# Fused RWKV-7 and attention blocks: moving the inversion's buffers and reordering the first loads of the recurrence

## The reference

```python
def step(S, inp):                       # per head, S is 64 x 64, for t = 1..512
    r_t, w_t, k_t, v_t, kk_t, kka_t = inp
    sa = jnp.einsum('bhvk,bhk->bhv', S, kk_t)
    S = (S * w_t[:, :, None, :] - sa[..., None] * kka_t[:, :, None, :]
         + v_t[..., None] * k_t[:, :, None, :])
    y_t = jnp.einsum('bhvk,bhk->bhv', S, r_t)
    return S, y_t
```

## Time and profile before

| what | value |
|---|---|
| median of 3 runs | 2405.3 us (2401.07 to 2406.37) |
| the profiled execution | 2402.93 us |
| its span of instructions | 2401.2 us |
| TensorE busy | 2141.7 us (89%) |
| VectorE busy | 1413.9 us (59%) |
| ScalarE busy | 1004.4 us (42%) |
| GpSimd busy | 264.8 us (11%) |
| mean granted TensorE clock | 0.955 |

### The profile page before, as it was taken

The page is one execution under the profiler, slowest core; times in us unless marked ns, Lnnn a source line. Parts: engine busy times, 40 slices in busy tenths (PEclk is TensorE's granted clock), DMA queues, the critical chain, the costliest instruction groups (busy, mean ns, idle before and its releaser), DMA issues.

```text
span 2401.2 us, 43608 instructions
## 1 busy us (share of the span) xinstructions
PE 2141.7 (89%) x16706; PEld 1664.0 (69%) x16706; DVE 1413.9 (59%) x2214; ACT 1004.4 (42%) x1768; POOL 264.8 (11%) x233
## 2 busy tenths in 40 slices
PE   3798999986888888799999999887989997999998
PEld 1576666765777776577888888575756685787876
DVE  6776776765656564446553555579855556434445
ACT  3454554443655565323222322331477424323233
POOL 2102000000222223100000000079100000000000
PEclk6899999997999999899999999899999999999998
DMA  3234445463333231332333333122211131333322
GB/s 100 70 123 133 137 142 160 154 157 84 82 81 88 67 73 38 93 91 79 87 96 98 94 94 95 58 79 61 79 53 36 40 100 53 87 97 96 96 87 80
DMA packets 395656, 217.19 MB, mean 90 GB/s; under 512 B 85104, under 2 KB 374280, under 8 KB 395272
## 3 DMA queue, kind: packets, MB, share of 16 engines
q1 hardware_dynamic: 394896, 215.13, 31.1%
q10 hardware_dynamic: 632, 0.21, 0.0%
HBM read 181.68 MB, written 33.62 MB: 90 GB/s over the span
## 4 chain that ended last, share of the span: by engine, by line
PE 62%; DVE 19%; ACT 10%; issue 6%; SPq 1%; DMA 1%; DVEq 0%; POOL 0%; ACTq 0%
PE bank L1460 16%; PE bank L1462 15%; PE bank L1461 15%; DVE w_lo L1605 4%; PE bank L512 3%; DVE dconv L1853 3%; ACT w_hi L1237 2%; PE bank L489 1%; DVE tmp L1654 1%; PE bank L520 1%; PE bank L435 1%; PE bank L421 1%; PE bank L867 1%; PE bank L463 1%; PE bank L858 1%
## 5 line engine op out<-in xcount | busy, mean ns | idle before, releaser
L1460 PE MATMUL bank<-xl,w_hi 128*128 128x512 f32 (+1 forms) x1696 | 685.2, 404 | 72.8 <-DVE xl L1610 40.8
L1461 PE MATMUL bank<-xl,w_lo 128*128 128x512 f32 (+1 forms) x1696 | 668.3, 394 | 0.0
L1462 PE MATMUL bank<-xl,w_hi 128*128 128x512 f32 (+1 forms) x1696 | 667.2, 393 | 0.0
L1237 ACT ACTIVATE w_hi<-w_raw 128x1024 fp32r<-128x1024 f32 (+2 forms) x298 | 301.6, 1013 | 438.7 <-PE bank L1462 434.1
L1460 PEld LDWEIGHTS bank<-xl,w_hi 128*128 128x128 f32 (+1 forms) x1696 | 320.5, 189 | 196.0 <-issue 62.3
L1605 DVE TENSOR_TENSOR w_lo<-w_raw,w_hi 128x1024 fp32r<-128x1024 f32 (+2 forms) x298 | 353.3, 1186 | 141.1 <-ACT w_hi L1237 129.7
L1462 PEld LDWEIGHTS bank<-xl,w_hi 128*128 128x128 f32 (+1 forms) x1696 | 321.1, 189 | 70.6 <-issue 2.4
L1461 PEld LDWEIGHTS bank<-xl,w_lo 128*128 128x128 f32 (+1 forms) x1696 | 321.6, 190 | 67.1 <-issue 4.4
L1460 PE MATMUL bank<-xh,w_hi 128*128 128x512 f32 x480 | 199.1, 415 | 49.8 <-DVE w_lo L1605 44.7
L1462 PE MATMUL bank<-xh,w_hi 128*128 128x512 f32 x480 | 193.0, 402 | 0.0
L1461 PE MATMUL bank<-xh,w_lo 128*128 128x512 f32 x480 | 192.6, 401 | 0.0
(11 more groups left out here) (310 smaller groups left out, 3091.2 us busy)
## 6 DMA issues: line engine op xcount, KB each, us to landing
w_raw<-in_a_w_in SPq DMA_DIRECT2D x64, 512.0 KB, 4.3
w_raw<-in_b_w_in SPq DMA_DIRECT2D x64, 512.0 KB, 4.0
w_raw<-in_w_ffn_up SPq DMA_DIRECT2D x44, 512.0 KB, 3.7
w_raw<-in_w_in SPq DMA_DIRECT2D x36, 512.0 KB, 3.6
w_raw<-in_a_w_out SPq DMA_DIRECT2D x16, 512.0 KB, 3.9
w_raw<-in_b_w_out SPq DMA_DIRECT2D x16, 512.0 KB, 3.8
w_raw<-in_w_ffn_down SPq DMA_DIRECT2D x16, 512.0 KB, 3.9
d_g<-sq SPq DMA_DIRECT2D x16, 256.0 KB, 2.1
```

Source lines behind the costliest of these rows:

```text
L1237: A(w_hi[0:rows, slot, 0:nkb, 0:ncol], w_raw[0:rows, slot, 0:nkb, 0:ncol], ACT.Copy).then_inc(s_hi, 1)
L1460: mm(outp, wh, xlo, start=start, stop=False)
L1461: mm(outp, wl, xhi, start=False, stop=False)
L1462: return mm(outp, wh, xhi, start=False, stop=stop)
```

## The change

The inversion's f32 buffer `nix`, and `nix16` and `inv2`, move out of the `hT` region into the second `xl` region. `tt` and `rhs` take their place in the `hT` region, where `nixlo16` and `w16` stay. ScalarE's wait for the last spill is removed, and VectorE's moves from its first instruction of the recurrence to its first write of `w16` (step 10 of pair 0). GpSimd's wait stays. In SP's queue the keys of pair 0 now stand between the two halves of its queries, and both halves of pair 1's queries move behind the values of pair 0 and `spill_mix(15)`.

```diff
         st_v = over("st_v", [P, 2, (NCH + 1) * C])
         sv = [over(f"sv{n}", [P, 2, NCH, 2, C]) for n in range(2)]
-        tt = [over(f"tt{n}", [P, 2, NCH, C]) for n in range(2)]
+        nix = [over(f"nix{a}", [P, NCH, C]) for a in range(2)]
+        nix16 = [over(f"nix16_{a}", [P, NCH, C], F16) for a in range(2)]
+        inv2 = [over(f"inv2_{a}", [P, 2, NCH, C], F16) for a in range(2)]
         st_pc = [over(f"st_pc{n}", [P, 2, NCH]) for n in range(3)]
-        rhs = over("rhs", [P, 2, C])
...
         assert spot == hT_at
-        nix = [over(f"nix{a}", [P, NCH, C]) for a in range(2)]
-        nix16, nixlo16, w16 = ([over(f"{n}_{a}", [P, NCH, C], F16) for a in range(2)]
-                               for n in ("nix16", "nixlo16", "w16"))
-
-        inv2 = [over(f"inv2_{a}", [P, 2, NCH, C], F16) for a in range(2)]
+
+        tt = [over(f"tt{n}", [P, 2, NCH, C]) for n in range(2)]
+        nixlo16, w16 = ([over(f"{n}_{a}", [P, NCH, C], F16) for a in range(2)] for n in ("nixlo16", "w16"))
+        rhs = over("rhs", [P, 2, C])
...
                     if when(t, PAIRS):
-                        if t == 0 and s == 0:
-                            act.wait_ge(s_spill, SPILL_MIX + SPILL_TILE * CI)
                         if s in (1, 3, 5, 7):
...
             dve.wait_ge(s_const, 3)
-            dve.wait_ge(s_spill, SPILL_MIX + SPILL_TILE * CI)
...
                         level = (s - S_LEVELS) // 2 + 1
+                        if t == 0 and level == 1:
+                            dve.wait_ge(s_spill, SPILL_MIX + SPILL_TILE * CI)
...
-            for half in range(2):
-                load_q(0, half)
+            load_q(0, 0)
             load_keys(0)
-            for half in range(2):
-                load_q(1, half)
+            load_q(0, 1)
             sp.wait_ge(s_unit, U_MIX + 4 * (CI - 1) + 3)
             load_values(0)
             spill_mix(CI - 1)
+            for half in range(2):
+                load_q(1, half)
             panel(U_OUT1 + 1, 1, i["a_w_out"][0], 0, KB, P)
```

## The result

| | before | changed |
|---|---|---|
| median of 6 runs each | 2405.49 us (2399.06 to 2407.77) | 2390.70 us (2386.92 to 2395.24) |
| the profiled execution | 2402.93 us | 2386.92 us |
| its span | 2401.2 us | 2385.2 us |
| TensorE busy | 2141.7 us | 2139.0 us |

The ratio of the times is 0.995, with a 95% interval of 0.9931 to 0.9969. The forecast was 2393 us with a range of 2387.5 to 2398.5.

A forecast was written before the change was run, and what follows sets the result against it. Bound: one queue and one landing decide 30.9 us into the recurrence. Terms 0 + 8.35 + 2.6 + 0 = 10.9 us gave 2392.0 against the profiled execution, 2394.4 against the median; forecast between them 2393 us, range 2387.5 to 2398.5.

The forecast's parts named there:

- The bound: From mix stage to recurrence, one queue and one landing decide 30.9 us; moving this hand-over moves the rest.
- The keys: Pair 0's key loads: first products start at about 534.4, 3.7 us earlier, and TensorE's 3.75 us idle stretch goes.
- The values: Pair 0's value loads: issued sooner, so TensorE's transposes start at 539.5, 8.35 us earlier, 2.3 us behind the last issue.
- The spill gate: ScalarE's start of the recurrence: no longer waiting for the last spill gains 2.6 us, because the values come next.
- VectorE's moved wait and pair 1's queries: VectorE's first `w16` and pair 1's query loads: both cost nothing, with covers of 16.7 us and 25 us.
- The clock: TensorE in pair 0's four groups: falls to half clock as before, 5.4 us a group, no gain counted.
- the clock comes back a group or two sooner: Rival in pair 0's groups: each group sooner gains 1.9 us; 2386.4 to 2391.1 including never falling, chance 0.25.
- The rival of the other side: Inversion at half clock: if all of it doubled, 16.7 us lost, 2411.1 us; chance 0.03.
- The size: Whole kernel: 10.9 us faster, forecast 2393 us, give or take half a microsecond 2390.5 to 2395, chance 0.50.
- half of the shift lost: Rival behind pair 0: something later does not move, giving 2399 us; shift partly or fully given back, chance 0.08.

The follow-up runs named there:

- buffers only: The changed kernel with SP's loads back in the old order, keeping the moved buffers and waits; 2399.18 us.
- waits kept: The changed kernel with ScalarE's and VectorE's waits for the last spill back ahead of their first recurrence instruction; 2395.59 us.
- order only: The kernel before with the new order of SP's loads, its buffers and waits for the last spill left as they were; 2396.68 us.
- second profile: The changed kernel profiled again, unchanged, in a later comparison; 2390.85 us.
- spills last: The changed kernel with pair 1's queries ahead of the last spills in SP's queue, behind pair 0's values; 2392.81 us.
- values-sooner run: The changed kernel with pair 0's values loaded ahead of the second half of its queries; 2387.89 us.
- filled groups: The kernel of the values-sooner run with dummy matmuls behind each set of pair 0's transposes; 2381.00 us.

## Why the prediction was right, point by point

**The bound.** The chain of one queue and one landing was read rightly. What moved the hand-over moved the end: the stretch lost 13.3 us, and the medians 14.8 and 10.4 us.

**The keys.** The products were expected at 534.4, 12.9 us behind the first query issue. They started 13.4 us behind it, and TensorE's idle time of 3.75 us fell to 0.54. The landing took 4.73 us from the last key issue (530.51 to 535.24) in place of 4.06.

**The values.** Expected were 8.35 us and a start of the transposes 18.0 us behind the first query issue. It was 18.3 us, with the landing at 2.3 us as taken. In other runs this landing took 2.2 to 3.65 us, so it is partly luck that the term came out so well. Between buffers only and the changed kernel, 27.8 and 20.1 us, the order is worth 7.6 us to the first copy.

**The spill gate.** The 2.6 us were 3.1 with the old order (before against buffers only) and 1.9 to 2.5 with the new one (changed against waits kept and order only). The sum of both, 10.9, was measured as 10.8 us.

**VectorE's moved wait and pair 1's queries.** Both were taken at nothing. In the changed kernel VectorE's first `w16` at 558.91 waited for TensorE, and pair 1's first products came 55.4 us behind the first query issue with no wait on a load. The cover of the spills, 16.7 us by the forecast, held in the run with the spills last, which spends 8 us of it.

**The clock.** This is the step that failed. I expected the four groups at half clock, 5.4 us each. In the changed kernel the clock came back at 547.2, before the third group's products, and the copies 1 to 4 took 2.8 us less (3.3 in the second profile). The term in the sum was nothing. This is the rival "the clock comes back a group or two sooner"; it had given 1.9 us a group. Together with the 10.9 us it would have given 2390 to 2391, which is where the median lies. The rival of the other side came too, in part: I had argued that the inversion would keep its full clock, and its first 3.6 us ran at half. The last part grew by 0.2 us only. What decides these moments is not settled. TensorE worked without a gap from 543.31 to 547.3 and the clock came back; before, it did the same work from 559.16 to 563.1 and the clock stayed. The Trainium skill, "TensorE: Matmul & The Clock Gate", Part 1, has the clock return after sustained work: the changed kernel's trace agrees, and in the kernel before it returned too, but only with the fourth group's end, at 568.95. So "sustained work" does not tell in which group it returns. In the run with the spills last, whose groups are the same work, it stayed at half through all four. That part of the gain stands in both profiles of the changed kernel and is not certain in any one execution.

**The size.** 2390.7 us against 2393, well inside the range. Two slips in the working did not matter: half a microsecond either way of 10.9 gives 2391.5 to 2394.9 us and not 2390.5 to 2395, and half of the shift lost gives 2398.5 us, the range's edge, and not 2399. The difference of the medians was 14.8 us in one comparison and 10.4 in another of the same two kernels, so the size of each part can be read only in the traces, and not in the times. That the first median lies on the sum with the clock's 2.8 us is partly luck, since what the later pairs and the rest gave or took was in no term.

## What to carry to other kernels

A wait that ended last hides the next one: here the spill gate opened 3 us later than the value gate. Taking it away alone was worth 3.1 us at ScalarE's first copy, where both parts gave 10.8; in time it was 5 us (anything from 0 to 7 by the interval), against 10 to 15. In a queue whose issues are the chain (0.6 us each), sort the loads by the time of their first reader, and send what nobody reads yet behind everything that somebody waits for; the best place for the values here was even one set further forward. When a change is small beside the spread of the runs, measure it between two events of the trace.

## What the runs showed of the hardware

A clock kept up in one stretch did not last into the next. With the groups at full clock (11.0 us for copies 1 to 4) the last part took 23.0, 24.0 and 26.0 us, with 3.5 to 7 us at half clock in the inversion. With the groups at half clock (16.1 us) it took 21.7 to 22.3 us. Only the two profiles of before kept the full clock in the inversion; the spills-last run, with its groups at half, was at half there too (0.91 in the mean of its 20 us), so the groups' clock does not decide it alone. Nor does TensorE's idle time in the groups: it was busy for 11.93 of the 16.14 us of the copies 1 to 4 before, 6.62 of 11.02 us in the values-sooner run, and 9.91 of 11.01 us in the filled groups, behind which the clock was at half for 7 us.

Transfers with short rows filled the transfer engines at half the rate. Three stretches of one microsecond of the kernel before, in a weight panel's load with rows of 512 bytes, in key and query loads with rows of 256 bytes, and in the spills with rows of 2 KB:

```profile
36.00:37.00 1.00, 0.28 (x1) 0.29 (x2) 0.90 (x2) 0.52 (x1) 1.00 (x1) 0.50 1.08 326
...
536.00:537.00 1.00, 0.00 (x0) 0.00 (x0) 0.00 (x0) 0.00 (x0) 0.00 (x0) 1.00 1.39 171
...
549.00:550.00 1.00, 0.79 (x4) 0.38 (x2) 0.00 (x0) 0.00 (x0) 0.00 (x0) 0.50 1.01 381
```

The share of the engines in use, in time of packets, is 1.08 for 326 GB/s, 1.39 for 171 GB/s and 1.01 for 381 GB/s. The first two are both loads, so the direction is not the reason. The Trainium skill, "DMA: Bandwidth & Descriptors", Specifications, puts the least transfer for full rate at 512 bytes, and this trace agrees, with rows of 512 bytes at nearly twice the rate of rows of 256.
